# Out-projection of a hybrid encoder layer: one plain float32 product per block in place of three products of rounded parts

## The reference, cut to what matters

```python
D_MODEL, SEQ, HEAD_DIM = 1024, 2048, 64          # one batch, one layer, float32
h = rmsnorm(x, g_norm_mix);  proj = h @ w_in      # queries, keys, values of two head groups
oa = neighbourhood_attention(qa, ka, va, rpb)     # 8 heads, 2-D windows with a position bias
ob = windowed_gqa_sink(qb, kb, vb, sink)          # 8 heads, windows of 128 with a sink
o = concatenate([rmsnorm(oa, g_out_na), rmsnorm(ob, g_out_swa)])   # 512 + 512 columns
x = x + o @ w_out                                 # the out-projection, 1024 x 1024
h = rmsnorm(x, g_norm_ffn)
x = x + (silu(h @ w_gate) * (h @ w_up)) @ w_down  # 2816 wide
return rmsnorm(x, g_final)
```

## Time and profile before

| | |
|---|---|
| median of 3 executions | 2251.94 us (2250.82 to 2252.31) |
| the profiled execution | 2250.96 us |
| its span, first to last instruction | 2249.2 us |
| around the span | 1.8 us |
| busy share PE / DVE / ACT / POOL | 98% / 64% / 41% / 14% |
| mean granted TensorE clock | 0.997 of full speed |

### The profile page before, as it was taken

One profiled execution on the slowest core, in us unless ns is written; L12 is line 12 of the kernel. 1 busy time (PEld: TensorE's weight loads), 2 busy tenths in 40 slices (PEclk: granted clock), 3 DMA queues, 4 the chain that ended last, 5 costly groups with the idle time before them and its releaser, 6 DMA issues.

```text
span 2249.2 us, 33191 instructions
## 1 busy us (share of the span) xinstructions
PE 2207.5 (98%) x11464; PEld 1816.7 (81%) x11464; DVE 1438.4 (64%) x2747; ACT 921.1 (41%) x1824; POOL 323.5 (14%) x304
## 2 busy tenths in 40 slices
PE   7999999999999999999999999999999999999998
PEld 6888888778877788877888888888888887888886
DVE  4412142399899878866666657665656578575676
ACT  4411121288888733343333335433333334131342
POOL 3370001154334100011112120000000002010200
PEclk9999999999999999999999999999999999999999
DMA  7473425789954375675555457323232286353544
GB/s 226 141 187 100 141 86 150 198 209 248 238 145 112 99 229 195 228 250 191 185 167 198 154 211 262 131 82 129 80 131 73 103 321 220 112 179 103 189 144 152
DMA packets 274677, 376.68 MB, mean 167 GB/s; under 512 B 15258, under 2 KB 182306, under 8 KB 269168
## 3 DMA queue, kind: packets, MB, share of 16 engines
q1 hardware_dynamic: 266528, 354.15, 49.3%
q0 software_dynamic: 5568, 11.87, 2.0%
q10 hardware_dynamic: 2448, 8.91, 1.4%
HBM read 237.77 MB, written 140.31 MB: 168 GB/s over the span
## 4 chain that ended last, share of the span: by engine, by line
PE 90%; DVE 4%; DMA 2%; issue 2%; ACT 1%; POOL 0%; SPq 0%; DVEq 0%; ACTq 0%
PE late_psum L2072 12%; PE late_psum L2074 12%; PE late_psum L2073 12%; PE late_psum L2103 6%; PE late_psum L2105 5%; PE late_psum L2104 5%; PE late_psum L1030 4%; PE late_psum L1008 3%; PE late_psum L533 3%; PE late_psum L1412 3%; PE late_psum L561 3%; PE late_psum L534 3%; PE late_psum L535 3%; PE late_psum L560 3%; PE late_psum L562 3%; PE late_psum L1414 3%
## 5 line engine op out<-in xcount | busy, mean ns | idle before, releaser
L2072 PE MATMUL late_psum<-ff_h,ff_ring 128*128 128x512 f32 x1232 | 480.4, 390 | 5.9 <-DVE ff_acts L1932 2.6
L2074 PE MATMUL late_psum<-ff_h,ff_ring 128*128 128x512 f32 x1232 | 480.0, 390 | 0.0
L2073 PE MATMUL late_psum<-ff_h,ff_ring 128*128 128x512 f32 x1232 | 479.9, 390 | 0.0
L2072 PEld LDWEIGHTS late_psum<-ff_h,ff_ring 128*128 128x128 f32 x1232 | 231.7, 188 | 55.6 <-DVE ff_acts L1932 3.5
L2073 PEld LDWEIGHTS late_psum<-ff_h,ff_ring 128*128 128x128 f32 x1232 | 231.7, 188 | 48.1
L2074 PEld LDWEIGHTS late_psum<-ff_h,ff_ring 128*128 128x128 f32 x1232 | 231.6, 188 | 48.1
L2103 PE MATMUL late_psum<-ff_d,ff_a 128*128 128x512 f32 x616 | 240.5, 390 | 6.5 <-DVE ff_x L1990 3.1
L2104 PE MATMUL late_psum<-ff_d,ff_a 128*128 128x512 f32 x616 | 239.7, 389 | 0.0
L2105 PE MATMUL late_psum<-ff_d,ff_a 128*128 128x512 f32 x616 | 239.7, 389 | 0.0
L1990 DVE TENSOR_TENSOR ff_x<-late_psum,ff_x 128x512 f32<-128x512 f32 x224 | 153.3, 689 | 120.6 <-PE late_psum L2105 120.1
L1888 DVE TENSOR_TENSOR ff_ring<-ff_raw,ff_ring 128x512 fp32r<-128x512 f32 x176 | 128.8, 733 | 102.7 <-ACT ff_ring L1765 102.6
(11 more groups left out here) (159 smaller groups left out, 4110.9 us busy)
## 6 DMA issues: line engine op xcount, KB each, us to landing
acts_scratch<-ff_acts SPq DMA_DIRECT2D x22, 1792.0 KB, 7.3
ff_a<-acts_scratch SPq DMA_DIRECT2D x24, 960.0 KB, 5.0
ff_raw<-in_w_gate SPq DMA_DIRECT2D x44, 512.0 KB, 3.8
ff_raw<-in_w_up SPq DMA_DIRECT2D x44, 512.0 KB, 4.0
ff_d<-down_scratch SPq DMA_DIRECT2D x21, 768.0 KB, 6.4
att_q_stack<-qk_scratch SPq DMA_DIRECT2D x56, 256.0 KB, 5.5
ffn_in_scratch<-mix_h_stage SPq DMA_DIRECT2D x8, 1792.0 KB, 6.3
ff_h<-ffn_in_scratch SPq DMA_DIRECT2D x14, 1024.0 KB, 8.6
```

Source lines behind the costliest of these rows:

```text
L2072: pe.matmul(out_bank, whi[:, k], hhi[:, :, k], start=(k == 0 and not onto), stop=False, skip_group_check=onto)
L2073: pe.matmul(out_bank, whi[:, k], hlo[:, :, k], start=False, stop=False, skip_group_check=onto)
L2074: last = pe.matmul(out_bank, wlo[:, k], hhi[:, :, k], start=False, stop=(k == 3), skip_group_check=onto)
```

## The change

The results are multiplied as they are loaded, and the scaled weights as they are scaled: one plain float32 product takes the place of the three. The rounding and subtracting of both operands go, with their buffers and semaphores. `o_in` takes the place of `o_split_lo` ahead of a tile's first product, `w_scaled` that of `w_lo_done`; `load_o(t)` now waits until all four products of tile t - 2 are done.

```diff
 gpsimd (attention phase), for k in range(KT):
-            raw, w_hi, w_lo = w_raw[:, k % 2, :], w_pool[:, k, :], w_pool[:, KT + k, :]
             pool.wait_ge(w_in[k % 2], 32 * (k // 2 + 1))
             wait_units(3 * k)
-            nc.gpsimd.tensor_scalar(raw, raw, gcol[:, k:k + 1], None, ALU.mult).then_inc(w_scaled, 1)
-            pool.wait_ge(w_scaled, k + 1)
-            wait_units(3 * k + 1)
-            nc.gpsimd.tensor_copy(w_hi, raw).then_inc(w_hi_done, 1)
-            pool.wait_ge(w_hi_done, k + 1)
-            wait_units(3 * k + 2)
-            nc.gpsimd.tensor_tensor(w_lo, raw, w_hi, ALU.subtract).then_inc(w_lo_done, 1)
+            nc.gpsimd.tensor_scalar(w_out_scaled[:, k, :], w_raw[:, k % 2, :], gcol[:, k:k + 1], None, ALU.mult) \
+                .then_inc(w_scaled, 1)
             if k + 2 < KT:
-                pool.wait_ge(w_lo_done, k + 1)
+                pool.wait_ge(w_scaled, k + 1)
                 load_w(k + 2)
...
 scalar and vector (attention phase):
-        stream(act, [...], {4: proj.last_high},
-               {UNITS + 1: lambda: mix.o_high(0)})
+        stream(act, [...], {4: proj.last_high})
-        stream(dve, [...],
-               {5: proj.last_low}, {UNITS + NORM_LAG - 1: lambda: mix.o_low(0)})
+        stream(dve, [...],
+               {5: proj.last_low})
...
 load_o:
         if t >= 2:
-            sp.wait_ge(o_split_lo, t - 1)
+            sp.wait_ge(mm_done, 4 * (t - 1))
             sp.wait_ge(o_squared, t - 1)
...
-    def o_high(t):
-        act.wait_ge(o_in[t % 2], 16 * (t // 2 + 1))
-        if t >= 2:
-            act.wait_ge(mm_done, 4 * (t - 1))
-        nc.scalar.copy(o_hi[:, t % 2], ot[:, t % 2]).then_inc(o_split_hi, 1)
-
     def o_squares(t):
         if t >= 1:
             act.wait_ge(sq_summed, t)
+        act.wait_ge(o_in[t % 2], 16 * (t // 2 + 1))
         nc.scalar.activation(sq[:], ot[:, t % 2], ACT.Square).then_inc(o_squared, 1)
...
-    def o_low(t):
-        dve.wait_ge(o_split_hi, t + 1)
-        nc.vector.tensor_tensor(o_lo[:, t % 2], ot[:, t % 2], o_hi[:, t % 2], ALU.subtract) \
-            .then_inc(o_split_lo, 1)
...
 product(t, i):
         if i == 0:
-            pe.wait_ge(o_split_lo, t + 1)
+            pe.wait_ge(o_in[t % 2], 16 * (t // 2 + 1))
         if t >= 1:
             pe.wait_ge(added, 4 * (t - 1) + i + 1)
         for k in range(4 * g, 4 * g + 4):
-            pe.matmul(mm[:, i, :], o_hi[:, t % 2, k, :], w_hi[:, k, cols], start=(k % 4 == 0), stop=False)
-            pe.matmul(mm[:, i, :], o_hi[:, t % 2, k, :], w_lo[:, k, cols], start=False, stop=False)
-            last = pe.matmul(mm[:, i, :], o_lo[:, t % 2, k, :], w_hi[:, k, cols], start=False,
-                             stop=(k % 4 == 3))
+            last = pe.matmul(mm[:, i, :], ot[:, t % 2, k, :], w_out[:, k, cols], start=(k % 4 == 0), stop=(k % 4 == 3))
         last.then_inc(mm_done, 1)
```

More of the change, by code:

```diff
@@ L656, in attention_phase @@
     negmax, total, rtotal = mem.att_stats
-    win_mask, sinks, gcol, w_raw, ident, w_pool = mem.win_mask, mem.sinks, mem.gcol, mem.w_raw, mem.ident, mem.w_pool
+    win_mask, sinks, gcol, w_raw, ident, w_out_scaled = mem.win_mask, mem.sinks, mem.gcol, mem.w_raw, mem.ident, mem.w_out
     rel, masks, biases = mem.rel, mem.masks, mem.biases
@@ L666, in attention_phase @@
     w_in, gains_in = [sem(f"w_out_in{i}") for i in range(2)], sem("gains_in")
-    w_scaled, w_hi_done, w_lo_done = sem("w_scaled"), sem("w_hi_done"), sem("w_lo_done")
+    w_scaled = sem("w_scaled")
     scored, shifted, exped = sem("scored"), sem("shifted"), sem("exped")
@@ L681, in weights_split @@
     def weights_split(eng):
-        eng.wait_ge(w_lo_done, KT)
+        eng.wait_ge(w_scaled, KT)
     def results_copied(eng):
@@ L917, in copy_turned, with scalar @@
         nc.scalar.copy(turned_buffer(kind, u)[:, 0:n], tp[:, u % 2, 0:n]).then_inc(pt_copied, 1)
-    def scalar(proj, mix):
-        stream(act, [(TURN_LAG, copy_turned), (1, set_sinks), (0, exp)], {4: proj.last_high},
-               {UNITS + 1: lambda: mix.o_high(0)})
+    def scalar(proj):
+        stream(act, [(TURN_LAG, copy_turned), (1, set_sinks), (0, exp)], {4: proj.last_high})
     def shift(kind, r, u):
@@ L978, in start, with vector @@
             dve.sem_inc(o_stored[i], 16)
-    def vector(proj, mix):
+    def vector(proj):
         stream(dve, [(NORM_LAG, invert), (0, shift), (NORM_LAG, normalise), (OUT_LAG, results)],
-               {5: proj.last_low}, {UNITS + NORM_LAG - 1: lambda: mix.o_low(0)})
+               {5: proj.last_low})
     def score(proj, kind, r, u):
@@ L1064, in __init__ @@
             self.psum = early.enter_context(nc.psum_tensor("late_psum", [P, 8, BANK], F32))
-        self.w_pool = self.at("w_pool", self.W_POOL, [P, 2 * KT, D], F32R)
+        self.w_out = self.at("w_out_scaled", self.W_POOL, [P, KT, D])
         self.rel = self.at("rel", 0, [P, 2, ROWS_REL * COLS_REL])
@@ L1101, in __init__ @@
         self.o_raw = self.at("mix_o_raw", self.O_TILES, [P, 2, KT, P])
-        self.o_hi = self.at("mix_o_hi", self.O_TILES + 8192, [P, 2, KT, P], F32R)
-        self.o_lo = self.at("mix_o_lo", self.O_TILES + 16384, [P, 2, KT, P], F32R)
         self.hs = self.at("mix_h_stage", self.MISC, [P, SEVEN, BANK])
@@ L1144 @@
 FIRST_SUMS = (5, 6)
-Mix = namedtuple("Mix", "load_o load_start o_high o_low product products_done bank_free norm_act norm_dve turn "
+Mix = namedtuple("Mix", "load_o load_start product products_done bank_free norm_act norm_dve turn "
                  "turn_copy sums store_h all_stored sync scalar vector tensor")
@@ L1159, in sem @@
         return nc.alloc_semaphore(f"mix_{name}")
-    w_hi, w_lo = mem.w_pool[:, 0:KT], mem.w_pool[:, KT:2 * KT]
-    ot, o_hi, o_lo, sq, sqs, xn, hs, gffn = (mem.o_raw, mem.o_hi, mem.o_lo, mem.sq, mem.sqs, mem.xn, mem.hs, mem.gffn)
+    w_out = mem.w_out
+    ot, sq, sqs, xn, hs, gffn = mem.o_raw, mem.sq, mem.sqs, mem.xn, mem.hs, mem.gffn
     oms, oinv, orms = mem.o_stats
@@ L1171, in mix_phase @@
     const_in = sem("const_in")
-    o_squared, o_split_hi, o_split_lo = sem("o_squared"), sem("o_split_hi"), sem("o_split_lo")
+    o_squared = sem("o_squared")
     sq_summed, o_stat, o_mean, o_inv, o_rms = (sem(n) for n in ("sq_summed", "o_stat", "o_mean", "o_inv", "o_rms"))
@@ L1287, in scalar @@
             if t + 1 < NT:
-                o_high(t + 1)
                 o_squares(t + 1)
@@ L1361, in vector @@
             if t + 1 < NT:
-                o_low(t + 1)
                 squares_sum(t + 1)
@@ L1433, in tensor @@
                 stats(1)
-    return Mix(load_o, load_start, o_high, o_low, product, products_done, bank_free, norm_act, norm_dve, turn,
+    return Mix(load_o, load_start, product, products_done, bank_free, norm_act, norm_dve, turn,
                turn_copy, sums, store_h, all_stored, sync, scalar, vector, tensor)
@@ L2230, in _ @@
             proj.scalar()
-            att.scalar(proj, mix)
+            att.scalar(proj)
             mix.scalar()
@@ L2238, in _ @@
             proj.vector()
-            att.vector(proj, mix)
+            att.vector(proj)
             mix.vector()
```

## The result

The changed kernel takes **2290.21 us** (median of 4, 2287.28 to 2291.22) against 2252.12 us for the kernel before measured beside it: a ratio of **1.017, 95% interval 1.0156 to 1.0183**, 38.1 us longer. The forecast was 2299, its stated range 2288 to 2310; the range of its sum alone was 2291 to 2310. The profiled execution takes 2290.95 us (span 2289.1).

The account below looks back on a forecast made before the run. TensorE, busy 98% of the span, was taken to bound the kernel. +49.1 - 0.9 - 1.0 = +47.2 us on the profiled 2250.96 gave 2298.2, so 2299 for the median; own range 2291 to 2310, stated 2288 to 2310.

Parts of the forecast that it names:

- The float32 product: TensorE, mix stage: 256 plain products at 872 ns replace 768 rounded ones; +49.1 us (+44.3 to +58.0).
- The first rival: Mix stage: float32 records move one column a cycle, 227 ns each; stage about 145 us, total 2199; chance 0.05.
- the lower bound: TensorE, one float32 block: bare cycles, 4 x 512 at 2.4 GHz, 853 ns.
- the part of the stage that was called unchanged: Mix stage: 22.9 us of transposes, sums of squares, last value products and starts between kinds stay as they are.
- The four passes: TensorE, mix stage: true FP32 takes four array passes; at the rounded step for each, the sum would be +58.0 us.
- VectorE and ScalarE in the mix stage: Removing 16 roundings of 1.04 us and 16 subtractions of 1.22 us costs nothing, as TensorE was busy throughout.
- End of attention: ScalarE's rounding ahead of a copy of transposed probabilities goes, so the first product comes earlier: -0.9 us (0 to -1.1).
- GpSimd, -1.0 (to -4.1): Attention: eight casts and eight subtractions go, VectorE stalls less; -1.0 us (0 to -4.1), counted from waits of TensorE's loads.
- The third rival: Attention follows VectorE: eight subtractions at 1.53 us give 12 us back instead of one, total 2288; chance 0.08.
- The new waits: Mix stage: the result load held until a tile's products are done is covered by 3.4 us at the median; 0.

Follow-up runs that it names:

- product_only: Kernel before with plain float32 product from unsplit operands; all roundings and subtractions still made, unused, and the low-part wait kept: 2296.09 us, ratio 1.0201.
- third_buffer: Changed kernel with a third buffer for the results, so their load starts a tile earlier: 2289.30 us, ratio 1.0173 to the kernel before.

## Why the prediction was right, and where it was off

- **The float32 product.** Two records for a product, two cycles a column: right. (The transposes, which the prediction calls float32 too, leave one record each, 128 for 16 tiles of eight; the sums of squares, plain products like the values', leave 64 for 32. They gave the step of a record, not the number of records.) The first rival (one cycle a column, 227 ns) is out with the 430 ns. The term was 5.4 us too large, +49.1 for +43.7. Of this 3.1 us is the step, 436 forecast and 430 measured. The prediction scaled 109 ns by columns and so took the record's fixed 3 ns four times; the lower bound, 427, was nearer. The other 2.3 us is the part of the stage that was called unchanged, 22.7 us before (196.8 less 174.1) and 240.5 - 220.1 = 20.4 after. Most of it was the price of going over from other kinds to rounded products: the first of the three lines has a mean of 403 ns, not 390, 3.3 us over its 256 records. The plain records' 595 is 3 ns over their median 592, 1.5 us over 512. That leaves 1.8 of the 2.3 us.
- **The four passes** that the Trainium skill, page "FP8 and Floating Point Precision", section "TensorE Precision Notes", gives to true FP32: the trace agrees with their number, 2 records of 2 cycles a column; which parts each one multiplies no trace shows. The sum at the rounded step, +58.0, is too high, as a pass of 512 columns takes 215 ns and not 227.
- **VectorE and ScalarE in the mix stage at nothing**: right, shown by product_only. The remark beside it, that 34 us lay there if the cover went, was too high by far for VectorE's part: 15 subtractions of 1.22 us would be 18, and 3.9 were measured; ScalarE's part was not tried. The first rival's price, a stage of 145 us paced by VectorE's busy time, fails for the same reason: 181 was measured with VectorE's subtractions out and a quicker product than it assumed. Busy time of the next engine is a lower bound, not a price.
- **End of attention, -0.9**: measured -0.6.
- **GpSimd, -1.0 (to -4.1)**: measured -4.7. This term failed: the 4.1 us of waits of TensorE's loads for one line were taken as its upper bound. Those waits fell by 3.4 us and the rounds by 4.7; waits of the moving passes, 3.6 us before and 0.4 after, were left out of the reading. The third rival (VectorE's stalls come back whole, 12 us) was wrong in size, but right that more was there than I took. The Trainium skill, page "GPSIMD Engine Reference", section "1. Specifications", says that GpSimd's interfaces to SBUF are shared with VectorE, with contention for some of VectorE's instructions; the trace agrees, with scalings of 1.98 us in place of 0.42. The price of the stalls goes by how the work is cut: in pieces it is gone.
- **The new waits at 0**: right, shown by third_buffer. The feed-forward part and the rest kept their length, 1282.3 and 1282.7 us.

The two misses, 5.4 us and 3.4 us (4.7 + 0.6 for 1.9), have one sign and make up the 8.8 us between 2299 and 2290.2. There is luck in the range. The sum's own ends, 2291 to 2310, miss 2290.2 by 0.8 us. It lies inside the stated 2288 to 2310 only because that was widened for the third rival, whose 12 us did not come.

## What to carry to other kernels

A plain float32 product cost TensorE 860 ns for 128 x 128 by 512, and three products of rounded parts 680. Where TensorE is the limit the splitting is the cheaper way, as long as the engines that do it stay inside TensorE's tempo, as they did here. Long GpSimd instructions beside a VectorE that is nearly full are worth cutting into pieces and spacing out: here pieces of 1 us and less took the whole loss away. An experiment that leaves an instruction out must keep the others as long as they were; look at their durations before reading its time. Before pricing what happens once the bound engine gets faster, take that engine's work out and look: here the stage fell by 9 to 16 us where busy times had promised 52.

## What the runs showed of the hardware that was not expected

- A plain float32 record has a smaller fixed part than a rounded one: 430 ns for two passes of 512 columns, against 226.7 ns for one. For each 512 cycles that is 215 against 227. Why the rounded one takes 12 ns more was not tried.
- GpSimd's eight casts of 1.09 us cost attention nothing alone, eight subtractions of 1.91 us cost 1.5 us alone, and casts with subtractions of 2.42 us cost 4.7. Cut into pieces, all of it cost nothing.
- With TensorE idle for 3.2 us its granted clock was 0.50 behind it (mean of the stage 0.77), and eight transposes took 1.97 us in place of 1.04, so an engine relieved of work ran slower in what was left.
